# A 1024 x 1024 mix product as seven block products over four pairs of output tiles

## The reference

```python
merged = gate_a * ya + gate_b * yb
x = x + jnp.einsum("bsd,de->bse", merged, mix_w_out[l])
h = rmsnorm(x, norm_ffn[l])
x = x + gdfn(h, ffn_w_up[l], ffn_dw_w[l], ffn_dw_b[l], ffn_w_down[l])
```

## Time and profile before

| | |
|---|---|
| median of 3 executions | 1298.08 us (1297.77 to 1298.23) |
| profiled execution: span, first to last instruction | 1295.9 us |
| its own time | not listed apart; it is an execution like the three |
| median less span | 2.2 us |
| TensorE busy | 1280.4 us, 99% |
| mean granted TensorE clock | 0.997 |

### The profile page before, as it was taken

One profiled execution on the slowest core, in us unless ns is written; L12 is line 12 of the kernel. 1 busy time (PEld: TensorE's weight loads), 2 busy tenths in 40 slices (PEclk: granted clock), 3 DMA queues, 4 the chain that ended last, 5 costly groups with the idle time before them and its releaser, 6 DMA issues.

```text
span 1295.9 us, 15702 instructions
## 1 busy us (share of the span) xinstructions
PE 1280.4 (99%) x5814; PEld 1063.7 (82%) x5814; DVE 987.1 (76%) x1117; ACT 457.9 (35%) x656; POOL 863.7 (67%) x567
## 2 busy tenths in 40 slices
PE   8999999999999999999999999999999999999997
PEld 8888888888888778888888888888888888888887
DVE  5898989999999684334767767677666679887975
ACT  6211221213244571011236444343343446433551
POOL 4536636666787833356848978878877876567861
PEclk9999999999999999999999999999999999999998
DMA  9411121214324372344412322332232249867923
GB/s 349 147 33 49 34 81 49 82 38 157 98 99 162 130 292 84 112 145 146 141 55 90 122 106 90 122 115 90 90 118 93 107 163 359 335 247 281 372 86 130
DMA packets 65384, 181.37 MB, mean 140 GB/s; under 512 B 5024, under 2 KB 13216, under 8 KB 61600
## 3 DMA queue, kind: packets, MB, share of 16 engines
q1 hardware_dynamic: 59776, 165.73, 35.3%
q10 hardware_dynamic: 5536, 14.69, 3.1%
HBM read 139.24 MB, written 41.16 MB: 139 GB/s over the span
## 4 chain that ended last, share of the span: by engine, by line
PE 90%; DVE 3%; issue 2%; ACT 2%; POOL 2%; DMA 1%; SPq 0%; POOLq 0%; DVEq 0%; ACTq 0%
PE ps L2128 30%; PE ps L2129 30%; PE ps L2130 30%; DMA cv<-in_x 1%; DVE h_lo L1823 1%; POOL w_lo L910 1%; PE ps L2192 0%; ACT cv L1049 0%; DVE cv L1814 0%; DVE res L2085 0%; ACT cv_r L1357 0%; DVE hi_f L1735 0%; PE ps L2182 0%; POOL w_lo L975 0%; DVE res L1905 0%
## 5 line engine op out<-in xcount | busy, mean ns | idle before, releaser
L2128 PE MATMUL ps<-h_lo,w_hi 128*128 128x512 f32 (+1 forms) x852 | 329.0, 386 | 3.0 <-DVE h_lo L1569 1.9
L2130 PE MATMUL ps<-h_hi,w_hi 128*128 128x512 f32 (+1 forms) x852 | 327.2, 384 | 0.0
L2129 PE MATMUL ps<-h_hi,w_lo 128*128 128x512 f32 (+1 forms) x852 | 327.2, 384 | 0.0
L2128 PEld LDWEIGHTS ps<-h_lo,w_hi 128*128 128x128 f32 x852 | 160.0, 188 | 37.3 <-DVE h_lo L1569 3.1
L2130 PEld LDWEIGHTS ps<-h_hi,w_hi 128*128 128x128 f32 x852 | 160.0, 188 | 31.7
L2129 PEld LDWEIGHTS ps<-h_hi,w_lo 128*128 128x128 f32 x852 | 160.1, 188 | 31.3
L837 POOL TENSOR_SCALAR w_hi<-raw 128x1024 fp32r<-128x1024 f32 x48 | 54.6, 1137 | 193.3 <-issue 136.7
L1649 DVE SCALAR_TENSOR_TENSOR ps<-tmp,par,ps 128x512 f32<-128x512 f32 x224 | 158.4, 749 | 0.0
L2128 PE MATMUL ps<-ga_r,w_hi 128*128 128x512 f32 (+1 forms) x383 | 148.6, 388 | 0.3 <-POOL w_lo L975 0.3
L2130 PE MATMUL ps<-cv_r,w_hi 128*128 128x512 f32 (+1 forms) x383 | 148.2, 387 | 0.0
L2129 PE MATMUL ps<-cv_r,w_lo 128*128 128x512 f32 (+1 forms) x383 | 148.2, 387 | 0.0
(11 more groups left out here) (274 smaller groups left out, 2603.7 us busy)
## 6 DMA issues: line engine op xcount, KB each, us to landing
raw<-in_wstream SPq DMA_DIRECT2D x66, 512.0 KB, 3.5
tmp<-in_wffn SPq DMA_DIRECT2D x13, 1024.0 KB, 4.8
g_kept<-res SPq DMA_DIRECT2D x21, 512.0 KB, 2.8
res<-in_wffn SPq DMA_DIRECT2D x10, 1024.0 KB, 4.8
ga_r<-g_kept SPq DMA_DIRECT2D x18, 512.0 KB, 6.9
h_lo<-g_kept SPq DMA_DIRECT2D x17, 512.0 KB, 6.4
g_kept<-raw SPq DMA_DIRECT2D x12, 512.0 KB, 2.8
tmp<-in_wffn SPq DMA_DIRECT2D x6, 704.0 KB, 5.4
```

The lines of the kernel that those rows point to most:

```text
L2128: nc.tensor.matmul(out, a_hi, b_lo, start=start, stop=False, skip_group_check=onto)
L2129: nc.tensor.matmul(out, a_lo, b_hi, start=False, stop=False, skip_group_check=onto)
L2130: return nc.tensor.matmul(out, a_hi, b_hi, start=False, stop=stop, skip_group_check=onto)
```

## The change

The mix product becomes a 2x2 block product too: output tiles in pairs (even, odd), the contraction in halves (tiles 0 to 3, tiles 4 to 7), positions in halves. Each of the four pairs takes seven products of 12 matmuls, 28 in all. `mix_op` numbers them: P1 for the four pairs, P2 for the four pairs, then P6, P4, P7 for each pair in turn, then P5, P5, P3, P3 for pairs 0 and 1 and again for 2 and 3. P1, P2, P6, P7 and P4 complete positions 0 to 511.

- **Tile sums**: T1 to T4 are made by VectorE as the merged tiles come (`mix_t1`, `mix_t3_t2_t4`), in place over `res` and in `cv`. High parts by ScalarE (`mix_t1_high`, `mix_t_high`), low parts by VectorE (`mix_t_low`, `mix_t1_low`), T2, T4 and T3 into `h_hi` and `h_lo`.
- **Weights**: for P1 and P2, quarters of 512 columns, two to a load, in `raw`. For the other five a block of 1024 KB per pair (W11, W12, W21, W22), in four places (`mix_block`), of which `mix_sums` on GpSimd makes S1 to S4. High parts by ScalarE (`mix_high`), low parts by GpSimd (`mix_low`), in a ring of four slots.
- **x** is loaded again in four quarters by SyncE (`load_x_again`), three of them only once the T sum that lies there has its low part. ScalarE issues no x loads.
- **Additions**: each product is added from its bank into every output tile that has it (`mix_add`): 44 additions of 512 columns instead of 16.
- **Squares** go to PSUM banks, the first of a half straight to `csum`. The first half's statistics stand inside `mix_product(P5, 1)`.
- ScalarE does `mix_high(P6, 2)` only after the first half's first five squares, and those after `P1 3 22` is added. From `mix_high(P5, 0)` on, high parts alternate with squares and the first half's norm; likewise on VectorE and GpSimd.
- The first up weights are split after P5 3 instead of after the last but one mix job.

```diff
-N_MIX = N_OUT + KT
-N_FFN = N_MIX + 2 * KT
+N_FFN = N_OUT + KT
...
+MIX_SLOTS = 4
+MIX_SUMS = ("S1", "S3", "S2", "S4")
+MIX_ADDS = (
+    "P2 0 11, P2 1 11, P1 0 11, P1 0 21, P1 1 11, P1 1 21, P1 2 11, P1 2 21, P1 3 11, P1 3 21, P2 2 11, P2 3 11, "
+    "P6 0 12, P1 0 12, P1 0 22, P1 1 12, P1 1 22, P4 0 21, P1 2 12, P1 2 22, P1 3 12, P1 3 22, P7 0 21, P7 0 22, "
+    "P6 1 12, P4 1 21, P7 1 21, P7 1 22, P6 2 12, P4 2 21, P7 2 21, P7 2 22, P6 3 12, P4 3 21, P7 3 21, P7 3 22, "
+    "P5 0 22, P5 1 22, P3 0 12, P3 1 12, P5 2 22, P5 3 22, P3 2 12, P3 3 12").split(", ")
...
+        def mix_block(i):
+            if i == 0:
+                return tmp[:, 0:BLOCK].rearrange("p (k n) -> p k n", k=4)
+            return four(*((hi_f, 0, 1), (lo_f, 0, 1), (cv, 0, 0))[i - 1])
...
+        def mix_bank(p, i):
+            if p == P1:
+                return bank(4 + i)
+            if p == P2:
+                return bank((2, 3, 0, 1)[i])
+            if p in (P5, P3):
+                return bank((2, 3, 0, 1)[i])
+            return bank((2, 0)[i % 2] + (p == P4))
...
+            load_mix_block(0, w_split, N_OUT + 2)
+            load_mix_quarter(0, 0, w_split, N_FFN - 1)
+            load_mix_quarter(1, 1, w_split, N_FFN)
+            load_x_again(0, 0, t_sum, 4 + KT // 2)
+            load_mix_quarter(2, 0, f_wlo, mix_op(P1, 1) + 1)
+            load_mix_block(1, w_used, N_FFN)
+            load_mix_quarter(3, 1, f_wlo, mix_op(P1, 3) + 1)
+            load_x_again(1, 1, t_lo, 5)
+            load_x_again(1, 0, t_lo, 6)
+            load_x_again(0, 1, t_lo, 7)
+            load_mix_block(2, w_used, N_FFN)
+            load_mix_block(3, f_used, mix_op(P1, 3) + 1)
+            for s, i in enumerate((1, 3)):
+                sp.wait_ge(f_wlo, mix_op(P2, i) + 1)
+                load_weights(N_FFN + s)
+            load_chunks(N_FFN // 2 + 1, NCHUNKS // 2)
...
+            def mix_sums(i):
+                w11, w12, w21, w22 = (mix_quarter(i, q) for q in range(4))
+                pool.wait_ge(mx_c[i], 16)
+                if i == 3:
+                    pool.wait_ge(f_used, mix_op(P1, 3) + 1)
+                pool.tensor_tensor(mix_s1(i), w21, w22, ALU.add).then_inc(f_sum, 1)
+                pool.tensor_tensor(w21, w11, w21, ALU.add).then_inc(f_sum, 1)
+                pool.wait_ge(f_sum, mix_summed(i, "S3"))
+                pool.tensor_tensor(w11, mix_s1(i), w11, ALU.add).then_inc(f_sum, 1)
+                pool.wait_ge(f_sum, mix_summed(i, "S2"))
+                pool.tensor_tensor(w12, w11, w12, ALU.add).then_inc(f_sum, 1)
+            def mix_low(p, i):
+                n = mix_op(p, i)
+                pool.wait_ge(f_whi, n + 1)
+                pool.tensor_tensor(mix_ring(w_lo, n), mix_weights(p, i), mix_ring(w_hi, n).bitcast(f32), ALU.subtract).then_inc(f_wlo, 1)
+            mix_sums(0)
+            for i in range(MP):
+                mix_low(P1, i)
+            mix_low(P2, 0)
+            mix_low(P2, 1)
+            mix_sums(1)
+            mix_low(P2, 2)
+            mix_low(P2, 3)
+            mix_low(P6, 0)
+            mix_low(P4, 0)
+            mix_low(P7, 0)
+            mix_sums(2)
+            mix_low(P6, 1)
+            mix_low(P4, 1)
+            mix_low(P7, 1)
+            mix_sums(3)
+            for i in (2, 3):
...
+            mix_low(P3, 2)
+            low_halves(n2[0], *span(0), None, (5,))
+            mix_low(P3, 3)
+            low_halves(n2[0], *span(0), None, (7,))
             for n in range(N_FFN, N_FFN + 2):
+                pool.wait_ge(f_used, FIRST_UP if n % 2 else mix_op(P5, 3) + 1)
...
+            def mix_high(p, i):
+                n = mix_op(p, i)
+                if p in (P1, P2):
+                    act.wait_ge(mx_a[2 * (p == P2) + i // 2], 16)
+                elif p == P4:
+                    act.wait_ge(mx_c[i], 16)
+                else:
+                    act.wait_ge(f_sum, mix_summed(i, {P5: "S1", P7: "S3", P6: "S2", P3: "S4"}[p]))
+                if n < GATE_OPS + MIX_SLOTS:
+                    act.wait_ge(w_used, N_FFN - 1 + i // 2)
+                else:
+                    act.wait_ge(f_used, n - MIX_SLOTS + 1)
+                act.activation(mix_ring(w_hi, n), mix_weights(p, i), ACT.Copy).then_inc(f_whi, 1)
...
+            merged_high(7)
+            mix_high(P2, 0)
+            mix_high(P2, 1)
+            mix_t_high("T2")
+            mix_high(P2, 2)
+            mix_t_high("T4")
+            mix_high(P2, 3)
+            mix_t_high("T3")
...
+                mix_high(P7, i)
+            act.wait_ge(mx_add, mix_added("P1 3 22"))
+            for j in range(5):
+                x1_square(0, j)
+            mix_high(P6, 2)
+            mix_high(P4, 2)
+            x1_square(0, 5)
+            mix_high(P7, 2)
...
+            def mix_t3_t2_t4(k):
+                n = 4 + KT // 2 + 3 * k
+                b12, b21, b22 = tile(res, k, HALF, SEQ), tile(res, 4 + k, 0, HALF), tile(res, 4 + k, HALF, SEQ)
+                dve.tensor_tensor(b12, b12, b22, ALU.subtract).then_inc(t_sum, 1)
+                dve.wait_ge(t_sum, n + 1)
+                dve.wait_ge(co_lo, 4 + k + 1)
+                dve.tensor_tensor(b22, tile(cv, k, HALF, SEQ), b22, ALU.add).then_inc(t_sum, 1)
+                dve.wait_ge(t_sum, n + 2)
+                dve.tensor_tensor(b21, b21, b22, ALU.subtract).then_inc(t_sum, 1)
+            merge(0)
+            for m in range(1, KT):
+                merge(m)
+                merged_low(m - 1)
+                if m <= KT // 2:
+                    mix_t1(m - 1)
+                else:
+                    mix_t3_t2_t4(m - 1 - KT // 2)
+            merged_low(KT - 1)
+            mix_t3_t2_t4(KT // 2 - 1)
...
+            mix_t_low("T2")
+            mix_t_low("T4")
+            mix_add("P2 0 11")
+            mix_add("P2 1 11")
+            mix_t_low("T3")
+            mix_add("P1 0 11")
+            mix_add("P1 0 21")
...
+            mix_t1_low()
+            mix_add("P6 1 12")
+            add_square2(0, 1)
+            add_square2(0, 2)
+            mix_add("P4 1 21")
+            add_square2(0, 3)
+            add_square2(0, 4)
...
-            def mix(t, ks=range(KT)):
-                if 0 in ks:
-                    pe.wait_ge(w_split, N_MIX + t + 1)
-                    pe.wait_ge(*((co_m, KT - 1) if t < 2 else (co_m, KT) if t < 4 else (x1_done, t - 3)))
...
+            def mix_product(p, i, first=True, ready=None, between={}):
+                n = mix_op(p, i)
+                pe.wait_ge(f_wlo, n + 1)
+                hi, lo = mix_ring(w_hi, n), mix_ring(w_lo, n)
+                for k in range(4):
+                    if ready:
+                        pe.wait_ge(*ready(k))
+                    mm = three(mix_bank(p, i), hi[:, k * P:(k + 1) * P], lo[:, k * P:(k + 1) * P],
+                               *mix_moving(PRODUCTS[p].partition("*")[2], k), first and k == 0, k == 3, not first)
+                    if k == 3:
+                        mm.then_inc(f_used, 1)
+                    if k in between:
+                        between[k]()
+            pe.wait_ge(f_post, gate_posted(GP - 1, "c12"))
+            for i in range(MP):
+                mix_product(P1, i, ready=(lambda k: (co_lo, k + 1)) if i == 0 else None)
+            for i in range(MP):
+                if i % 2 == 0:
+                    pe.wait_ge(co_m, KT - 1 + i // 2)
+                mix_product(P2, i, ready=(lambda k: (co_lo, 4 + k + 1)) if i == 0 else None)
+            for i in range(MP):
+                pe.wait_ge(mx_add, mix_added(f"P2 {2 * i} 11" if i < 2 else f"P7 {i - 2} 22"))
+                if i == 0:
+                    pe.wait_ge(t_lo, 4 + 1)
+                mix_product(P6, i)
+                pe.wait_ge(mx_add, mix_added(f"P2 {2 * i + 1} 11" if i < 2 else f"P4 {i - 2} 21"))
+                if i == 0:
+                    pe.wait_ge(t_lo, 4 + 2)
+                mix_product(P4, i)
+                if i == 0:
+                    pe.wait_ge(t_lo, 4 + 3)
+                pe.wait_ge(mx_add, mix_added(f"P6 {i} 12"))
+                mix_product(P7, i, False)
+            pe.wait_ge(t_lo, 4 + 4)
+            for a in (0, 2):
+                pe.wait_ge(mx_add, mix_added(f"P7 {2 + a // 2} 22"))
+                mix_product(P5, a)
+                mix_product(P5, a + 1, between={0: lambda: variance2(0), 3: lambda: broadcast2(0)} if a == 0 else {})
+                pe.wait_ge(mx_add, mix_added(f"P5 {a} 22"))
+                mix_product(P3, a, False)
+                pe.wait_ge(mx_add, mix_added(f"P5 {a + 1} 22"))
+                mix_product(P3, a + 1, False)
```

More of the change, by code:

```diff
@@ L952, in _ @@
                 pool.tensor_tensor(lo, r, hi.bitcast(f32), ALU.subtract).then_inc(w_split, 1)
[L954 to L957, removed]
+            splits(N_OUT // 2 + 1, N_FFN // 2)
+            def mix_sums(i):
[9 more added lines that the diff above has]
+                pool.tensor_tensor(w12, w11, w12, ALU.add).then_inc(f_sum, 1)
@@ L1314, in _, with merged_high @@
```

(26 more changed lines are left out.)

331 lines of the change are left out of this document (234 added, 97 removed).

## The result

The changed kernel takes 1304.64 us (median of 4, 1304.47 to 1305.16) against 1297.97 for the kernel before (4 runs beside it): a ratio of 1.005, 95% interval 1.0038 to 1.0063, so 6.7 us slower. Forecast were 1304.9 and +6.8. The span went from 1295.9 to 1302.6 us.

The account below looks back on a forecast made before the run. TensorE's matmul count was taken to bound the kernel: 10.9 us saved against 17.1 of stalls and 0.6 of restarts, so 1298.08 + 6.8 = 1304.9 us. Own range 1301 to 1308.5; 8 in 10, 1294 to 1309.5.

Parts of the forecast that it names:

- step 1: Stage start: VectorE's half-tile sums and low parts alternate with GpSimd's operations, ending at 572.5 instead of 565.5 alone.
- Step 2: P2 2 waits behind T2's parts and starts at 578.0, stall 5.2; P2 3 stalls 0.6, P2 0 0.1.
- Step 3: T3's low part ends at 584.7; VectorE's additions behind it hold P7 0 until 591.5, stall 2.1.
- Step 4: Block 2 lands at about 592.5; P6 1 waits until 598.8, stall 4.6; P4 1 stalls 0.6, P6 2 2.1.
- rival C: Block 2 lands 1 us later, T1's low part goes before P6 1's: + 1 + 2.2, 1308.1 us; chance 0.12.
- 8 to 9: Total slowdown in us if, by the skill's DMA figure, block 2 landed 1 to 2 us later.
- Step 5: Stage end: norm work and the up-weight split hold the up-projection, stall 1.6 with hand-over; 0.2 before P3 3.
- The sum: Whole stage: stalls 17.1 and restarts 0.6 make 17.7, less 10.9 saved: 6.8 us slower at the first up job.
- The hand schedule: Engine queues worked from operation prices through the mix stage, giving when each product starts and stalls; 6.8 us slower.
- A: Engines do not hinder each other in the half-tile sums: 6.6 - 10.9 = -4.3, 1293.8 us; chance 0.15.
- B: Half the VectorE and GpSimd contention: stalls 8 to 14, time 1295.5 to 1300.7 us; chance 0.12.
- D: Clock falls to 1.2 GHz behind the long gaps, two slow products behind each: + 5.4, 1310.3 us; chance 0.06.

Follow-up runs that it names:

- experiment 1: Changed kernel with GpSimd's four weight sums of block 1 moved behind its low part for P7 of pair 0: 1301.60 us, ratio 1.0026 to the kernel before.
- experiment 6: Changed kernel with 16 extra unused matmuls on TensorE before P2 2 and 16 before P6 1: 1304.10 us, ratio 1.005 to the kernel before.
- experiment 4: Changed kernel with SyncE's loads of weight blocks 2 and 3 ahead of the three x reloads: 1299.36 us, ratio 1.0012 to the kernel before.
- experiment 5: Changed kernel with VectorE's T1 low part after the additions of P7 1 instead of before that of P6 1: 1303.42 us, ratio 1.0046 to the kernel before.
- experiment 2: Changed kernel with block 1's sums behind P7 0's low part and T1's low part after P7 1's additions: 1299.03 us, ratio 1.0007 to the kernel before.
- experiment 3: Changed kernel with ScalarE's high parts of P2 2 and P2 3 before T2's: 1303.64 us, ratio 1.0043 to the kernel before.
- experiment 7: Changed kernel with block 1's sums behind P2 3's low part, plus the edits of experiment 3 and experiment 4: 1297.84 us, ratio 1.0 to the kernel before.
- experiment 8: Changed kernel with experiment 7's three orders, T1's low part later, T3's low part and the first up-weight split earlier: 1294.63 us, ratio 0.9976 to the kernel before.

## Why the prediction was right

- **Start and step 1.** The last half-tile sum was to end at 572.5, and it did (570.79 + 1.66). The exclusion that the earlier trace rows showed on four operations holds for these, and experiment 1 shows it by taking the partner away. GpSimd was not without a break, as the prediction had it: its low parts waited 0.86 and 0.66 for ScalarE's high parts, one of VectorE's sums met no turn of GpSimd (562.74), and the first sum ended 1.3 later than forecast (562.7 instead of 561.4); by low part 7 the two agreed again within 0.2. The price of a 512-wide sum alone, 0.55, was too low: in experiment 1 they start 0.71 to 0.73 apart. With a turn of GpSimd between, they start 1.70 to 1.81 apart, where 1.75 were taken.
- **Step 2.** P2 2 at 578.0: measured 578.00, a wait of 5.11 (5.2 forecast). The 0.6 before P2 3 was not paid: most of the product before it ran at the lower clock, so TensorE came that much later. The 0.1 before P2 0 was not paid either.
- **Step 3.** T3's low part was to end at 584.7: the additions follow it at 584.46. That held by luck, since this turn was a tie: had it fallen as in experiment 6, it would have ended 1.1 us earlier, and about 1 us of the stage with it. P7 0 was to start at 591.5: 591.21. The wait is 0.46 instead of 2.1, for the reason given in step 2.
- **Step 4.** Block 2 at 592.5: 592.47, so the 7.7 that was taken without a row held. (A load 1 us later would by rival C's sum have cost 3.2, so the "8 to 9" that the prediction gives for a slower load should have been about 10.) P6 1 at 598.8: 599.05, wait 4.84 (4.6). The wait before P6 2 is 1.23 instead of 2.1. Experiment 4 shows the cause, the place in SyncE's queue.
- **Step 5.** The end's wait is 1.15 instead of 1.6, and the first up matmul is at 651.70 where 652 was said.
- **The sum.** Stalls and restarts of 17.7 were forecast and 17.1 measured, less 10.9: 6.2 in the stage. Its start is 0.10 later than before, and between the first up matmul and the FFN's first product 0.13 more came on, so the shift there is 6.45. The kernel ended 6.7 later.
- **The hand schedule elsewhere.** It gave the times of six of the eight experiments within 0.6 us; it missed by 1.0 in experiment 5 and by 1.4 in experiment 1, whose slip experiment 2 explains.
- **Rivals.** A and B needed sums that end earlier; out by the trace. C did not happen in the changed kernel, but by 0.2 us only: P6 1's low part starts at 597.65 and T1's at 597.83, which is luck at the precision of this schedule. The turn came in experiment 1, where it cost 2.1 before P6 1. D's drop did happen, behind both gaps, but for 11 matmuls in all, less than the one product (12 matmuls) behind each that the prediction called free, and not the two that would have cost 5.4. The Trainium skill's "TensorE: Matmul & The Clock Gate" (Part 1) was right on the drop; its price here was near nothing by experiment 6. So the right total holds errors that cancel: waits of 13.6 instead of 17.1, most of the difference before P7 0, P6 2, P2 3 and P4 1, against 2.2 of slow matmuls and 0.7 more of late starts. The two are not independent: where the next product waits for another engine anyway, as P6 2 does in experiment 6, what the slow clock takes is taken off that wait. This is why the starts of the products were right though the prediction had no slow matmuls.

The claim that the added operations cost nothing where a product runs meanwhile also held: VectorE's busy time rose by 35 us and GpSimd's by 7, and the only losses are at the places named.

The Trainium skill says that VectorE instructions with two SBUF inputs contend with GpSimd ("GPSIMD Engine Reference", Specifications); that page gives no price. These traces agree and give one: a turn of the other engine, which adds 1.0 to 1.1 us to a 512-wide sum of 0.69.

## What to carry to other kernels

When work is taken off the bounding engine, list what the others must deliver in front of each of its jobs and lay the orders of all queues side by side before counting the gain; a saving of 10.9 us turned into a loss of 6.7 and, with the same arithmetic in another order, into a gain of 3.2. Loads that wait for nothing belong ahead of loads that wait, and VectorE operations with both inputs in SBUF are to be scheduled with GpSimd's as if the two were one engine. A gap closed by one order alone can come back where the next late chain ends, as in experiment 3 (1.0 us kept of 4.3), while the order that sits in the last link keeps its gain, as in experiment 4 (5.3 us). So the last link (here VectorE's sums and the queue of block 2) has to move too.

## What the runs showed of the hardware that was not expected

- The granted clock fell behind waits shorter than those of the changed kernel: 4.24 and 3.41 us in experiment 3 and 2.42 in experiment 7, where it is 0.57 between 580.4 and 583.0 and seven matmuls start 0.43 apart. Behind the waits of 1.62 us and less in experiment 7 they stayed 0.23 apart. In experiment 8 the first two starts behind the gap of 4.47 us are still 0.30 and 0.35 apart, and only the next is 0.43. Such a stretch held 5 to 11 matmuls; 11 in experiments 2 and 3, behind waits of 5.70 and 3.41 us.
- When operations of VectorE and GpSimd start within 0.01 us of each other, either may have the first turn: T3's low part of 2048 columns took 3.42 us in the changed kernel and in experiment 4, and 2.28 in experiments 1, 2 and 6.
